# Attention scores ordered by the height of their products, and a residual addition put ahead of a weight split

## The reference

```
for i in range(DEPTH):
    h = rms_norm_2(x, norm1_g[i])
    ...
        mix, q_mem = gmlp_mixer(h, ...)        # layer three
        mix, q_mem = mla_mixer(h, positions, ...)   # layer four
    mem_out = memory_attention(q_mem, mem_k, mem_v, mem_qn_g[i], mem_kn_g[i])
    x = x + jnp.concatenate([mix, mem_out], axis=-1) @ w_out
    x = x + hierarchical_moe(rms_norm_2(x, norm2_g[i]), ...)
```

```
    q = jnp.concatenate([q[..., :NOPE_DIM], rope(q[..., NOPE_DIM:], positions)], axis=-1)
    k = jnp.concatenate([k[..., :NOPE_DIM], rope(k[..., NOPE_DIM:], positions)], axis=-1)
    o = causal_block_attention(q, k, v)
```

## Time and profile before

| | |
|---|---|
| median of 3 runs | 1597.28 us (1597.07 to 1597.29) |
| profiled execution, its own time | 1595.46 us |
| its span in the trace | 1593.7 us |
| PE busy | 1510.5 us, 95% of the span |
| DVE busy | 1313.9 us, 82% |
| ACT busy | 1040.7 us, 65% |

### The profile page before, as it was taken

The page is one execution under the profiler, slowest core; times in us unless marked ns, Lnnn a source line. Parts: engine busy times, 40 slices in busy tenths (PEclk is TensorE's granted clock), DMA queues, the critical chain, the costliest instruction groups (busy, mean ns, idle before and its releaser), DMA issues.

```text
span 1593.7 us, 21383 instructions
## 1 busy us (share of the span) xinstructions
PE 1510.5 (95%) x7230; PEld 1235.7 (78%) x7230; DVE 1313.9 (82%) x1970; ACT 1040.7 (65%) x1523; POOL 104.8 (7%) x204
## 2 busy tenths in 40 slices
PE   6999999979999999989979999999899889999998
PEld 4887877857878778768768888888787678888886
DVE  5778899877878998866678999988785579999897
ACT  3555677745646777646447877777675457777775
POOL 4020000030205000020200000000000000000000
PEclk9999999989999999999979999999999979999999
DMA  8535699965437999755538999999442429999996
GB/s 278 179 114 172 197 332 348 325 210 176 162 125 232 315 343 327 257 174 155 172 112 278 360 360 359 364 328 355 162 143 80 136 67 352 358 360 361 358 334 226
DMA packets 307792, 400.27 MB, mean 251 GB/s; under 512 B 16716, under 2 KB 221260, under 8 KB 307428
## 3 DMA queue, kind: packets, MB, share of 16 engines
q1 hardware_dynamic: 298500, 382.00, 72.4%
q0 software_dynamic: 9184, 16.91, 3.7%
HBM read 397.80 MB, written 1.05 MB: 250 GB/s over the span
## 4 chain that ended last, share of the span: by engine, by line
PE 76%; DVE 16%; ACT 4%; issue 2%; DMA 1%; DVEq 0%; ACTq 0%; SPq 0%; POOLq 0%
PE bank L648 21%; PE bank L649 21%; PE bank L650 21%; DVE w_lo_at L2046 5%; PE bank L796 2%; PE bank L665 1%; ACT w_hi_at L1446 1%; PE bank L823 1%; PE bank L964 1%; PE bank L770 1%; DVE uc_at L2601 1%; PE bank L771 1%; DVE x_at L2093 1%; PE bank L1368 1%; PE bank L1367 1%
## 5 line engine op out<-in xcount | busy, mean ns | idle before, releaser
L2046 DVE TENSOR_TENSOR w_lo_at<-raw_at,w_hi_at 128x1024 fp32r<-128x1024 f32 (+1 forms) x730 | 853.8, 1212 | 96.0 <-ACT w_hi_at L1446 83.9
L1446 ACT ACTIVATE w_hi_at<-raw_at 128x1024 fp32r<-128x1024 f32 (+1 forms) x730 | 726.2, 1046 | 135.9 <-PE bank L650 70.6
L648 PE MATMUL bank<-w_hi_at,xs_hi_at 128*128 128x512 f32 x800 | 323.1, 404 | 3.3 <-DVE xs_lo_at L2446 1.6
L650 PE MATMUL bank<-w_hi_at,xs_lo_at 128*128 128x512 f32 x800 | 314.3, 393 | 0.0
L649 PE MATMUL bank<-w_lo_at,xs_hi_at 128*128 128x512 f32 x800 | 314.0, 393 | 0.0
L648 PE MATMUL bank<-w_hi_at,t_hi_at 128*128 128x512 f32 (+3 forms) x528 | 210.7, 399 | 17.8 <-DVE t_lo_at L2058 9.0
L650 PE MATMUL bank<-w_hi_at,t_lo_at 128*128 128x512 f32 (+3 forms) x528 | 203.5, 385 | 0.0
L649 PE MATMUL bank<-w_lo_at,t_hi_at 128*128 128x512 f32 (+3 forms) x528 | 203.2, 385 | 0.0
L648 PEld LDWEIGHTS bank<-w_hi_at,xs_hi_at 128*128 128x128 f32 x800 | 150.4, 188 | 35.8 <-issue 2.4
L650 PEld LDWEIGHTS bank<-w_hi_at,xs_lo_at 128*128 128x128 f32 x800 | 150.5, 188 | 34.4
L649 PEld LDWEIGHTS bank<-w_lo_at,xs_hi_at 128*128 128x128 f32 x800 | 150.8, 189 | 29.3
(11 more groups left out here) (517 smaller groups left out, 1740.4 us busy)
## 6 DMA issues: line engine op xcount, KB each, us to landing
raw_at<-in_moe_w_dram SPq DMA_DIRECT2D x192, 512.0 KB, 5.5
raw_at<-in_moe_w_gate_dram SPq DMA_DIRECT2D x128, 512.0 KB, 5.9
raw_at<-in_moe_w_up_dram SPq DMA_DIRECT2D x128, 512.0 KB, 7.5
raw_at<-in_moe_w_down_dram SPq DMA_DIRECT2D x128, 512.0 KB, 6.1
raw_at<-in_w_in_dram SPq DMA_DIRECT2D x40, 512.0 KB, 5.7
raw_at<-in_a_w_in_dram SPq DMA_DIRECT2D x20, 512.0 KB, 4.6
raw_at<-in_w_out_dram SPq DMA_DIRECT2D x16, 512.0 KB, 4.4
raw_at<-in_ple_wg_dram SPq DMA_DIRECT2D x16, 512.0 KB, 5.3
```

The source lines that it names most:

```text
L648: pe.matmul(out, ah, bh, start=start, stop=False, skip_group_check=loose)
L650: return pe.matmul(out, al, bh, start=False, stop=stop, skip_group_check=loose)
L1446: act.activation(WH[:, s.part(), a], RAW[:, s.slot(), a], ACT.Copy).then_inc(hi_half[i], 1)
L2046: dve.tensor_tensor(WL[:, s.part(), a], RAW[:, s.slot(), a], WH[:, s.part(), a].bitcast(F32), ALU.subtract).then_inc(split_half[i], 1)
```

## The change

In `scores(r)` the four products over 128 rows are issued first and then the four over 64 rows, where before each cell's two stood together. The number of products and their sizes stay. The accumulation's start and stop flags are set to fit. In `end_mixer` of layers three and four, DVE's split of unit H is moved from ahead of `add_and_measure(L, 0)` to behind it, ahead of the low parts of the turned half. ACT's program, the loads and the rest of PE's program stay as they were.

```
             def scores(r):
                 a, b = 4 + 2 * (r % 2), 5 + 2 * (r % 2)
                 claim(a, b)
-                for qb, at0 in ((1, 0), (0, T)):
-                    w, q_ = P * (qb + 1), slice(qb * P, qb * P + P)
-                    for i, bank in enumerate((a, b)):
-                        part = slice(64 * i, 64 * i + 64)
-                        out = BK[bank][:, at0:at0 + w]
-                        pe.matmul(out, QTN[:, 2 * r + i, q_], KTN[:, 2 * r + i, 0:w], start=True, stop=False)
-                        ins = pe.matmul(out, QTR[part, r, q_], KTR[part, r, 0:w], start=False, stop=True)
+                cells = [(qb, at0, P * (qb + 1), i, bank) for qb, at0 in ((1, 0), (0, T)) for i, bank in enumerate((a, b))]
+                for qb, at0, w, i, bank in cells:
+                    q_ = slice(qb * P, qb * P + P)
+                    pe.matmul(BK[bank][:, at0:at0 + w], QTN[:, 2 * r + i, q_], KTN[:, 2 * r + i, 0:w], start=qb == 1, stop=False,
+                              skip_group_check=True)
+                for qb, at0, w, i, bank in cells:
+                    q_, part = slice(qb * P, qb * P + P), slice(64 * i, 64 * i + 64)
+                    ins = pe.matmul(BK[bank][:, at0:at0 + w], QTR[part, r, q_], KTR[part, r, 0:w], start=False, stop=qb == 0,
+                                    skip_group_check=True)
                 ins.then_inc(*scores_ready.tick((mla, r)))
...
                 for strip in range(2):
                     used(first, unit + strip)
                     add_and_measure(L, strip)
+                    if strip == 0:
+                        split()
                     turn_raw(key, (2 * strip, 2 * strip + 1), H_AT[L], GAIN[L], (4, 5, 4, 5))
...
             turn(("mixed_b", 2), 4, TH[:, 4:8, :], TL[:, 4:8, :], banks=(6, 7))
             route_low(2)
             split()
-            split()
             split()
             split()
             split()
...
             turn(("heads_b", 3), 4, TH, TL, banks=(5, 7))
             route_low(3)
-            split()
             split()
             split()
             end_mixer(3, first, 16)
```

## The result

| | before | changed |
|---|---|---|
| median, us | 1597.28 (1597.07 to 1601.95, 4 runs) | 1584.63 (1582.59 to 1585.57, 4 runs) |
| ratio, 95% interval | | 0.9919 (0.9903 to 0.9935) |
| profiled execution, us | 1595.46, span 1593.7 | 1585.57, span 1583.8 |

The changed kernel is faster, by 12.65 us between the medians, where the prediction said 9.8. The two profiled executions are 9.89 us apart, nearly the forecast. So the sum is right from trace to trace and short from median to median; the experiments are mostly about the difference.

The account below looks back on a forecast made before the run. PE, busy 95% of the span, was taken to bound the kernel. Additions (3.35 and 1.8 us) and scores (1.14 and 3.5) sum to 9.8 us off the median 1597.28, giving 1587.5; range 1585.0 to 1591.0.

Parts of the forecast that it names:

- the sum: Whole kernel: 3.35 + 1.8 + 1.14 + 3.5 = 9.8 us less, 1587.5 from the median.
- Scores: Layer four's scores: fewer changes of height and overlapping 64-row products, 1.14 us gained in one pair of rounds, 3.5 in the other.
- the price of a change: Layer four's scores: each change between 128-row and 64-row products costs PE 0.20 us.
- the second pair: Rounds 2 and 3 of layer four's scores: DVE waits for the scores, so the whole 3.5 us are kept.
- the first pair: Rounds 0 and 1 of layer four's scores: 1.14 us kept, the other 2.4 us become new waits of PE.
- The clock did not fall behind them: Rival: the clock falls in PE's new waits, rounds 0 and 1, losing 1.6 us; 8.2 gained, 1589.1; chance 0.22.
- The rival without overlap: Layer four's 64-row products do not run at once: 2.2 instead of 3.5 us, 8.5 in all, 1588.8; chance 0.13.
- the rival that the height is not the cause: The 0.20 us is paid per cell or accumulation, so scores gain little: 1592.1; chance 0.08, with other losses of that gain.
- Additions: End of mixer: PE's wait ahead of the turn of x goes; second addition 3.35 us earlier in layer three, 1.8 in four.
- The step that failed: Layer three's clock fall priced at 1.57 us, none in layer four, and 9.8 us taken from a median 1.8 higher.
- The rival of chance: Rival to the clock, named with the experiments: the gain beyond the sum is the chance of four runs; no chance given.
- The range: Whole kernel: 1585.0 to 1591.0 us, taking in 1589.1 plus nearly 2 us of clock, and 2.5 below.

Follow-up runs that it names:

- the scores alone: The kernel before with only the order of products in layer four's scores changed, the splits as before: 0.9956 (0.9943 to 0.9969), median 1591.05 us.
- the filled wait: The kernel before with eight unused 512-column products ahead of PE's turn of x in layers three and four: 0.9991 (0.9980 to 1.0002), median 1595.79 us.
- the additions alone: The kernel before with only H's split moved behind the first addition, layers three and four: 0.9948 (0.9933 to 0.9964), median 1588.61 us.
- same half: The changed kernel with each round's 64-row products sorted by half of the partitions, even head's then odd head's: 0.9927 (0.9908 to 0.9947).

## Why the prediction was right, and where it was not

**Scores.** Right. The round at 2.35 us (forecast 2.4), the price of a change 0.20, the second pair shorter by 8.25 − 4.69 = 3.6 us (forecast 3.5) and all of it kept, and the first pair cut to 1.05 (forecast 1.14) with waits within 0.15 us of those named. The clock did not fall behind them in the changed kernel's own traces. The overlap of the 64-row products is real and belongs to the two halves of the partitions, as all of them in one half showed; that they alternate, which the prediction pointed to, is not needed. The rival without overlap falls, and the rival that the height is not the cause falls.

**Additions.** Right. Against the earlier trace rows the second addition stands 10.23 − 6.47 = 3.76 us closer to E's end in layer three (forecast 3.35; H's split and the low parts followed each other more tightly than I had added them up) and 8.65 − 6.47 = 2.18 in layer four (forecast 1.8).

**Trace to trace.** 3.76 + 2.18 + 1.05 + 3.6 would be 10.6. The starts of layer four's second addition are indeed 1276.95 − 1266.53 = 10.42 us apart, and the ends 9.89. In parts that the change doesn't touch the traces shift against each other by 1 to 2.5 us either way, with the places where the clock falls. That two single executions of kernels that each spread over several microseconds lie 9.89 us apart, so near the forecast, is in part luck.

**The step that failed** is the last one of the sum: "Of these 1.57 are clock ... in layer four it did not behind the same wait", taken as what the kernel does, and then "from the median, 1.8 higher". One trace shows one execution, and there the clock had fallen behind one of two like waits. Over three traces that have these waits it fell behind four of six (both in one trace, the one of layer three in the trace of before, the one of layer four with the scores alone). In the ten traces of kernels without the waits it never fell there. What the runs show in place of that term: by that count the two waits cost 4/6 × 2 × 1.57 = 2.1 us of clock in an execution, where the sum had 1.57: an estimate from six cases. That the base lay 1.8 us above the profiled execution was the hint: this was a trace with less time at the lower clock than most (a mean granted clock of 0.980, where the executions together have 0.9787), and I took the difference as a constant of the base. So the removed waits were under-priced by 0.5 us; the rest of what was missing is also less time at the lower clock, but which falls it came from isn't shown.

How much that is: each execution has a span and a mean granted clock, and twice what the clock lacks to 1, times the span, is its time at the lower level of 1.2 GHz. Over the 68 executions of the kernel before in the three longer series it is 67.9 us in the mean, over 22 of the changed kernel 60.9, so 7.0 us less, give or take 2.7. Twelve with the filled wait have 64.8, twelve with the scores alone 62.3, eleven with the additions alone 60.4. What a microsecond at the lower level costs: in the trace matmuls of 512 columns start 0.43 us apart behind the turn (807.40, 807.83, 808.26) and 0.23 us apart ahead of it (802.21, 802.44), so at most half a microsecond; within the executions of one kernel, times rise by 0.35 us for each. Seven make 2.4 to 3.5 us, where the sum had 1.57.

The longer series gives the whole its size. The mean of the 68 executions before is 1597.8, that of the 22 changed 1586.1: 11.8 us, give or take 1.2. Of the forecast's 9.8, 8.2 were not clock; 8.2 and 3.5 are 11.7. Less time at the lower clock thus accounts for the whole, by the upper of the two prices, and for all but 1.2 us by the lower. The two waits of the turns, by the count above, account for 0.5 of the 2 us that the sum was short. The rival of chance has its part too: the four runs of the result, at 1584.63, lay 1.5 us below the mean of all 22, and a like series gave 1586.53.

**The range.** Its lower end allowed 2.5 us for a fall avoided; it left out that a median of four executions of a kernel whose single executions spread over 10 us moves by a microsecond or more by itself.

**What stays open.** Which falls make up the 7 us at the lower level. The filled wait took back about 3 of them, give or take 3. And the waits of the turns can't be all: with the scores alone both waits are still there, and yet the time at the lower level is 67.9 − 62.3 = 5.6 us less than before, give or take 3.6. A fall between 1192 and 1204 us, ahead of the scores, is in four of five traces of kernels in which at least one part of the change is missing and in one of nine of those that have both. But the scores come behind it and can't be its cause; sorted by what stands ahead of it, it is in three of the four traces with layer three's split in its old place and in two of the ten with the split moved. In so few traces that may be chance, and no experiment was made on it.

## What to carry to other kernels

Group products by their height, and share those over 64 rows out over both halves of the partitions: a change of height costs 0.20 us each time here, and the two halves work side by side in any order within a group. A short wait of TensorE in front of its own work can cost more than its length, since the clock may fall behind it, and not in every execution: count such waits in several traces before pricing them, and add the chance of a fall at each. A difference of two traces is a difference of two single executions, so compare terms in the traces and the whole in long series; if the profiled execution lies apart from the median, ask for the mean granted clock of both before carrying the difference along as a constant. When a gain turns into a new wait, look at once for what the waiting engine's partner does first; here one split moved behind the maxima took back 2.6 us more.

## What the runs showed of the hardware

Products over 64 rows run side by side in the two halves of the partitions even where several of one half come first: a round's eight matmuls take 0.86 us in both orders, and 1.50 us when all are in one half. That the halves need not alternate I had not expected; by the starts of the run "same half" it means, as inferred there, that products of one half begin ahead of products of the other that come before them in the program. The Trainium skill (TensorEngine Tiling (Array Packing), Key Properties) lets different tiles work in parallel; the 0.86 against 1.50 us agree.

With eight unused products in a wait of 2.08 us the granted clock stayed at 1.00 in both layers of the one trace taken, where it fell in four of six such waits without them.

The executions of one unchanged kernel spread over 10 us, 0.6%, with a mean granted clock from 0.976 to 0.985. The Trainium skill (TensorE: Matmul & The Clock Gate, What's actually happening) puts the penalty of the clock's ramp at under 1% of a typical kernel's span. Here, with every fall counted, the lower level holds 68 us of 1596; if each cost 0.35 to 0.5 us, that would be 1.5 to 2.1%. This is an estimate and rather too high: much of the time lies behind the routers, where PE waits anyway (busy 4.21 of 7.00 us from 817 to 824 in the trace before), and its price there was not measured.
